# Tuning a streaming-encoder layer on eight cores: v's weights once per tile, and another tile for each first copy of the weights

## The reference, cut to what matters

```python
xn = rmsnorm(x, g_pre_mix)
z = xn @ w_in                       # (B,T,1024) @ (1024, 6*1024)
xa, ga, u, v, gates = jnp.split(z, [...], axis=-1)
xc, conv_new = causal_conv(xa, conv_prev, conv_w, conv_b)
hseq, h_last = rglru(xc, h0, w_a, b_a, w_x, b_x, lam)
o_a = (hseq * jax.nn.gelu(ga)) @ w_br_a                       # branch A
vn = layernorm(jax.nn.gelu(v), ln_g, ln_b)
o_b = (jax.nn.gelu(u) * spatial_gate(vn, w_s, b_s)) @ w_br_b  # branch B
g_a, g_b = jnp.split(jax.nn.sigmoid(gates), 2, axis=-1)
x = x + rmsnorm((g_a * o_a + g_b * o_b) @ w_out, g_post_mix)
gate, up = jnp.split(rmsnorm(x, g_pre_ffn) @ w_ffn_in, 2, axis=-1)
x = x + rmsnorm((jax.nn.silu(gate) * up) @ w_ffn_out, g_post_ffn)
```

## Time and profile before

| | |
|---|---|
| median of 3 runs | 2137.91 us (2136.51 to 2145.68) |
| the profiled execution | 2138.31 us |
| its span, slowest core (6) | 2136.8 us |
| spans of the eight cores | 2119.7 to 2136.8 us |
| TensorE busy | 2057.6 us (96%) |
| VectorE, ScalarE, Pool busy | 1127.0, 970.5, 548.4 us |
| the 16 DMA engines busy | 39.8% (casting queue) and 38.1% (SP's queue) |
| granted TensorE clock, mean | 0.990 |

### The profile page before, as it was taken

How to read it: one execution, slowest core, us unless ns; L and a number is a source line. 1 busy time by engine, 2 the same in 40 slices (tenths; PEclk the granted TensorE clock), 3 DMA queues, 4 the chain that set the end, 5 groups by cost and what they waited for, 6 DMA issues and landing times.

```text
span 2136.8 us, 35683 instructions; the slowest of 8 cores (2119.7 to 2136.8 us)
## 1 busy us (share of the span) xinstructions
PE 2057.6 (96%) x10775; PEld 962.6 (45%) x10775; DVE 1127.0 (53%) x1610; ACT 970.5 (45%) x1531; POOL 548.4 (26%) x920
## 2 busy tenths in 40 slices
PE   5998999998999999999999999999999999999998
PEld 2444445443444444444444444444444444444543
DVE  4863775236762377514774167722785248732542
ACT  3763873116741277313781157611784127711311
POOL 3323431223322243113431133211331022200200
PEclk9999999999999999999999999999999999999999
DMA  9998778889889998898988799858859466544353
GB/s 188 209 174 183 168 149 149 142 176 238 170 150 179 208 238 176 168 172 224 240 173 170 174 252 233 201 156 221 279 162 226 155 204 211 166 150 153 126 163 131
DMA packets 157768, 395.77 MB, mean 185 GB/s; under 512 B 18704, under 2 KB 18768, under 8 KB 157584
## 3 DMA queue, kind: packets, MB, share of 16 engines
q0 software_dynamic: 36368, 131.42, 39.8%
q1 hardware_dynamic: 121216, 262.08, 38.1%
HBM read 471.29 MB, written 53.54 MB: 246 GB/s over the span
## 4 chain that ended last, share of the span: by engine, by line
PE 87%; DMA 7%; issue 2%; DVE 1%; ACT 1%; POOL 1%; SPq 0%; DVEq 0%; ACTq 0%; POOLq 0%
PE ps L574 86%; DMA mring<-wsc 3%; DMA fring<-wt 3%; DMA xres<-xp 1%; PE ps L789 1%; DMA xpre<-xp 1%; DVE XC L888 0%; ACT junk L580 0%; DMA yp<-xres 0%; POOL stats L672 0%; ACT xsb L580 0%; POOL stats L675 0%; DVE hnT L792 0%; ACT xcb L580 0%; DVE xres L816 0%
## 5 line engine op out<-in xcount | busy, mean ns | idle before, releaser
L574 PE MATMUL ps<-hnT,fring 128*128 128x512 bf16 (+2 forms) x2880 | 631.5, 374 | 2.0 <-DVE hnT L792 1.6
L574 PE MATMUL ps<-xnT,mring 128*128 128x512 bf16 x2400 | 562.6, 380 | 3.6 <-DMA mring<-wsc 1.6
L574 PEld LDWEIGHTS ps<-hnT,fring 128*128 128x128 bf16 x2880 | 278.3, 98 | 330.2 <-issue 3.7
L580 ACT ACTIVATE T<-ps 128x512 f32<-128x512 f32 x247 | 146.1, 596 | 560.3 <-PE ps L574 534.5
L574 PEld LDWEIGHTS ps<-xnT,mring 128*128 128x128 bf16 x2400 | 229.5, 98 | 267.6 <-issue 11.9
L574 PE MATMUL ps<-fring,ffT 128*128 128x512 bf16 (+1 forms) x1424 | 325.5, 379 | 0.0
L1137 DVE SCALAR_TENSOR_TENSOR T<-T,ps 128x512 f32<-128x512 f32 x120 | 82.5, 688 | 381.6 <-PE ps L574 381.6
L632 POOL DMA_DIRECT2D fring<-wt x196 | 110.8, 565 | 509.5 <-PE ps L574 459.3
L1342 DVE SCALAR_TENSOR_TENSOR sgt<-sgt,ps 128x512 f32<-128x512 f32 (+2 forms) x182 | 122.2, 673 | 220.9 <-ACT sgt L580 204.4
L580 ACT ACT_TABLE_LOAD x164 | 210.4, 1283 | 26.4 <-PE ps L574 22.3
L574 PEld LDWEIGHTS ps<-fring,ffT 128*128 128x128 bf16 (+1 forms) x1424 | 139.3, 98 | 167.0 <-issue 0.4
(11 more groups left out here) (158 smaller groups left out, 2013.3 us busy)
## 6 DMA issues: line engine op xcount, KB each, us to landing
mring<-wsc SPq DMA_DIRECT2D x444, 256.0 KB, 5.9
fring<-wt POOLq DMA_DIRECT2D x196, 512.0 KB, 8.5
fring<-wsc SPq DMA_DIRECT2D x222, 256.0 KB, 3.2
mring<-wt POOLq DMA_DIRECT2D x53, 512.0 KB, 11.0
wsc<-fring SPq DMA_DIRECT2D x47, 512.0 KB, 8.8
xpre<-xp SPq DMA_DIRECT2D x30, 512.0 KB, 12.9
xres<-xp SPq DMA_DIRECT2D x29, 512.0 KB, 13.6
yp<-xres SPq DMA_DIRECT2D x29, 512.0 KB, 7.7
```

The lines of the kernel that those rows point to most:

```text
L574: P.op("pe", lambda e: e.matmul(out, lhsT=lhsT, rhs=rhs, start=start, stop=stop), reads=reads, writes=writes, cost=max(27.0, n / 2.4 + 2.5))
L580: P.op("act", lambda e: e.activation(out=out, in_=in_, func=func, **kw), reads=reads, writes=writes, cost=165.0 + 0.833 * n + 93.0 * aps + ...
```

## The change

In all tiles one `v_get(h)` now serves all subtiles: the former `s_v0` is the only `s_v`. The two float32 blocks that `T8` has no room for lie in `gsT` (blocks 0 to 3, seen as float32) instead of `sgt`. After the first tile, half 0 of v comes with XA 0 and half 1 with XA 4. `VM` is written by two operations of 512 columns a subtile instead of one of 1024. In `STORE_AT`, GTA and BRA are stored at use 0, in the first tile; XA, GA, V and BRB at use 1, in the second; GTB at 2; U and OUT at 3; the ffn pairs one or two uses earlier than before. The loads of `ln_g` and `ln_b` name all of `hnT` as written.

```diff
 def STORE_AT(q):
     pid = PAIRS[q][0]
     if pid >= W_FO:
-        return 3 if pid < W_FO + 8 else 4
+        return 1 if pid < W_FO + 8 else 2
     if pid >= W_FG:
         j = pid - W_FG
-        return 2 if j < 2 else 3 if j < 6 else 4 if j < 14 else 5
+        return 1 if j < 2 else 2 if j < 4 else 3 if j < 12 else 4
     if pid >= W_OUT:
-        return 4
-    if pid >= W_BRB or W_GTB <= pid < W_BRA:
         return 3
-    if pid >= W_BRA:
-        return 1
-    if pid >= W_GTA:
+    if W_GTA <= pid < W_GTB or W_BRA <= pid < W_BRB:
+        return 0
+    if W_GTB <= pid < W_BRA:
         return 2
-    return 0
+    if W_U <= pid < W_V:
+        return 3
+    return 1
...
+        gsF = gsT[:].rearrange("p c t -> p (c t)").bitcast(F32)
...
-                def s_v(p, h):
-                    got = v_get(h)
-                    for ss in range(2):
...
-                def s_v0(h, s):
+                def s_v(h, s):
                     if s == 0:
                         S["v", h] = v_get(h)
                     got = S["v", h]
...
-                    slot = (lambda n: (T8[:, n, :], ("T8", n)) if n < 4 else (sgt[:, n - 4, :], ("sgt", n - 4)))
+                    slot = (lambda n: (T8[:, n, :], [("T8", n)]) if n < 4 else
+                            (gsF[:, (n - 4) * 512:(n - 3) * 512], [("gsT", 2 * (n - 4)), ("gsT", 2 * (n - 4) + 1)]))
                     where = [slot(s), slot((4, 5, 0, 1)[s])]
...
-                    vu = [(0, 0), (0, 1), (1, 0), (1, 1)]
                     for c in range(NCH):
                         add(U, lambda c=c: s_xa(c))
-                        if c % 2 == 0:
-                            add(2 * U, lambda c=c: s_v(*vu[c // 2]))
+                        if c % 4 == 0:
+                            for s in range(NSUB):
+                                add(U, lambda c=c, s=s: s_v(c // 4, s))
```

More of the change, by code:

```diff
@@ L723, in row_loads @@
                 cdma(lambda e: e.dma_start(out=hist_s[:], in_=sc_in), writes=[("hist_s",)], after=P.mark())
-                cdma(lambda e: e.dma_start(out=lng_bc[0:64, :], in_=ln_g.partition_broadcast(64)), writes=K_hnT[0:2], nbytes=1 << 18, after=P.mark())
-                cdma(lambda e: e.dma_start(out=lnb_bc[0:64, :], in_=ln_b.partition_broadcast(64)), writes=K_hnT[2:4], nbytes=1 << 18, after=P.mark())
+                cdma(lambda e: e.dma_start(out=lng_bc[0:64, :], in_=ln_g.partition_broadcast(64)), writes=K_hnT, nbytes=1 << 18, after=P.mark())
+                cdma(lambda e: e.dma_start(out=lnb_bc[0:64, :], in_=ln_b.partition_broadcast(64)), writes=K_hnT, nbytes=1 << 18, after=P.mark())
                 dve(64, lambda e: e.memset(wsT[64:128, :, 0:64], 0.0), (), [("wsT",)])
@@ L958, in s_v0 @@
                     v_unit(got, lambda k: xnT[:, k, s * 128:(s + 1) * 128], 128, b, [("xnT", s)])
-                    v_evac(128, b, where[h][0], [where[h][1]], s, h)
+                    v_evac(128, b, where[h][0], where[h][1], s, h)
                     if h == 1:
-                        v_norm(128, s, [(where[x][0], [where[x][1]], VM[:, 2 * s + x, :], [("VM", 2 * s + x)]) for x in range(2)])
+                        v_norm(128, s, [(where[x][0], where[x][1], VM[:, 2 * s + x, :], [("VM", 2 * s + x)]) for x in range(2)])
                 def s_vs_out():
@@ L1243, in mixer @@
                         for s in range(NSUB + 1):
-                            add(U, lambda h=h, s=s: s_v0(h, s))
+                            add(U, lambda h=h, s=s: s_v(h, s))
                         if h == 0:
```

## The result

The changed kernel takes 0.9885 times the time of the kernel before, with a 95% interval of 0.984 to 0.993. Its profiled execution took 2117.59 us and another one 2115.32 us; the profiled execution before took 2138.31 us, so the two profiled ones differ by 20.7 us. The forecast was 2120 us, in a range of 2102 to 2145. Executions that were disturbed (a lower granted clock on one die) are left out of all comparisons, here three of the five of the change.

What follows compares the result with a forecast made beforehand. The prediction took TensorE, busy 96% of the span, as the bound, with only its stalls and the half clock behind them recoverable. Its terms -9 - 9 - 4 + 4 = -18 gave 2120 us, range 2102 to 2145.

Steps and rivals of the forecast that it cites:

- the forecast's own case: Whole kernel: -18 us to 2120 us, with its own range of 2110 to 2128; chance 0.45.
- First tile, -9: First tile: eight stores less remove two TensorE waits for casts and the half clock behind the second; -9 us.
- no wait for a cast before 60 us: Sign that the forecast is right: TensorE has no such wait in the first tile, and no clock of 0.57 there.
- v's loads, -9: Tile starts: v's fetches fall from 4 to 2 a tile, removing waits for v's weights and their clock loss; -9 us.
- the 4 that the prediction set: Sign that the forecast is right: TensorE's waits for `wsc` loads fall from 10.6 to under 4 us.
- Seams of tiles 3 and on, -4: Tiles 4 to 6: a lighter DMA queue may bring x's rows sooner, making tile 5's start like tile 6's; -4 us.
- The test of tile windows that lose under 2 us: Sign that the forecast is right: tile windows from tile 4 on lose under 2 us.
- Tile 1, +4: Tile 1: 12 pairs become casts with stores in its first 100 us, adding DMA work; +4 us, between -3 and +18.
- At nothing: `VM` by two operations, ScalarE's waits for `VM`, Pool's fewer casts and SP's added issues: all priced at no time.
- The rule on casts starved by VectorE: Tile 1: Pool-issued casts delayed by certain VectorE operations, an estimated 4 us more for 8 added casts; left out.
- The second rival: TensorE arrives earlier and waits for `xcb` and `xsb` instead; -4 us, 2134 us; chance 0.23.
- The third rival: Tile 1 runs short of weights, with Pool issuing for both rings in order; slower, 2166 us; chance 0.15.

Runs made afterwards that it cites:

- the table alone: The kernel before with the new `STORE_AT` only, v still fetched twice a tile; ratio 0.9979 to the kernel before (0.9967 to 0.9991), 4.5 us.
- v alone: The change with the old `STORE_AT`, so only v fetched once per tile; 2118.39 and 2118.13 us, beside a median of 2136.5 for the kernel before.
- the ring of 8: The change with 8 instead of 10 buffers in the mixer's ring, same bytes; ratio to the kernel before 0.9979, the change beside it 0.992.
- the second fetch back: The change with v's weights fetched again for subtiles 2 and 3 in all tiles after the first; ratio 1.0027 to the kernel before, profiled 2138.57 us.
- x's rows sooner: The change with tile 1's rows of x loaded earlier in the first tile; ratios 0.9904 and 0.9895 to the kernel before, beside 0.992 of the change.

## Why the prediction was right

The sum was -18 and the profiles differ by 20.7. The sign, the size and the forecast's own case came true. In part that is luck, since two misses cancel: tile 1, forecast at +4, came out at -2.5, and tiles 2 to 6, forecast at -13 (v's loads and the seams), at -8.9.

- **First tile, -9.** It gave 8.5 us here, 9.1 with the table alone, and 7.2 of it went when the stores came back. The stall at 52.2 us with its clock is gone, as the step said. The test "no wait for a cast before 60 us" failed by the wait of 3.42 us at 18.3 us. The rows of x of tile 1, 3.60 and 6.75 us with 18 us at a clock of 0.67, are what is late next. More than half of that loss was in the kernel before as well, and the step had not priced it.
- **v's loads, -9.** The term priced the starts of tiles 2 to 4. v alone gave 8.9 us in these tiles, as forecast, but 18 in all, with 3.1 more in the first tile, 1.9 in tile 1 and 4.2 in tile 5. In the whole change tiles 2 to 4 gave only 3.1: the table alone costs 2.6 there, and TensorE still waits 3.4 us in tile 4, for `xcb` and `xsb`. So the term is right for v alone, too large for the whole change in its own place, and too small for what v is worth: taking the single fetch out again cost 21 us by the profiled executions, 23 in tiles 1 to 4. The waits for `mring<-wsc` are 3.2 us, under the 4 that the prediction set, though with 2.1 on the other ring. That the fetch costs by what it keeps from being fetched ahead fits the ring of 8 and tile 3, but the bytes were not parted from it.
- **Seams of tiles 3 and on, -4.** Tiles 4, 5 and 6 gave -1.2, 5.2 and 0.6, together 4.6, and the place is the one named: tile 5's start became like tile 6's. But either part of the change does that by itself. The reason given, x's rows sooner on a lighter queue, was not shown. The test of tile windows that lose under 2 us holds for tiles 5 and 6, where TensorE waits 1.1 and 1.2 us, and not for tile 4.
- **Tile 1, +4.** The table alone lengthens it by 5.0 us, so this step's size was right for the table. What the step left out is v: in the whole change tile 1 is 2.5 shorter, and with the second fetch back it is 6.8 longer again. The share rose from 0.84 to 0.97, near the 1.0 forecast, and no wait for `mring<-wt` is in core 6's list.
- **At nothing.** VectorE's busy time rose by 3.8 us and ScalarE's fell by 1.4, with no cost to be seen; `VM` is in no wait of the list above.
- **The rule on casts starved by VectorE** (the Trainium skill, page "SBUF — State Buffer", section "SBUF: two separate sides"). By it tile 1 would have been longer by an estimated 4 us more, 8 in all for the table. The table alone cost 5.0 where the sum without the rule said 4, so it was not needed. No run tests it.
- **The second rival** wanted the waits to return under other names. That happened in part at the end of the first tile, and again with x's rows sooner; in the change itself `xcb` and `xsb` over ScalarE stayed at 24 us.
- **The third rival** needed over 15 us of waits in tile 1; the window of 203 to 326 us loses 1.0. It was not near: even with 8 casts more in tile 1 TensorE waited 1.6 us there.

Open: v alone and the table alone give 18 and 4.5 us, which is no more than the interval of the whole allows; by the stages they overlap in tile 5. How the second fetch's cost divides between DMA time, ring buffers and the planner's order was not settled in any tile. In tile 1 there is one thing more: the second fetch is no cast there, as was expected (the casts stay 205), but reads copies of v's weights that have only just been stored.

## What to carry to other kernels

A load that is made twice can be worth more than the waits that bear its name: here 18 us by itself, where all waits for loads into that ring were 10.6. Put it back by itself to price it, and look at the start of a tile, where the DMA engines are full and loads land late; in tiles with a share of 0.57 to 0.71 it was worth nothing. Where latencies stand in a row, removing one only shows the next.

Where a planner sets the order, each edit is two: what you changed, and the order that comes with it. Two looks guard against this. Look in the trace where the added work really ran before you read what it cost. And count the work on both sides of a boundary before you compare two stages.

## What the runs showed that was not expected

On the second chip the kernel before took 2177 to 2181 us (medians) instead of 2137. Windows of the change there, core 4, 1110 to 1150 us:

```profile
1110.00:1120.00 10.00, 10.00 (x48) 4.51 (x47) 4.21 (x7) 8.18 (x12) 2.28 (x6) 1.00 1.01 228
1120.00:1130.00 10.00, 10.00 (x42) 4.27 (x41) 8.36 (x11) 8.06 (x11) 4.41 (x5) 0.88 0.85 192
1130.00:1140.00 10.00, 10.00 (x46) 4.47 (x45) 5.97 (x10) 4.95 (x8) 0.88 (x3) 0.83 0.71 150
1140.00:1150.00 10.00, 10.00 (x57) 4.91 (x56) 7.57 (x11) 8.00 (x10) 4.46 (x5) 1.00 0.60 119
```

TensorE is busy all of each 10 us, and the granted clock reads 0.88 and 0.83 for a while: a lower clock with no idle time ahead of it, unlike the half clock behind the stalls. It is not a mix of the two levels of the first chip: the trace has a third value, 0.812. Core 4 had 28 such stretches, up to 15.1 us long; its mean clock was 0.959. On the first chip no core has one. The change is worth 0.992 of the time there and 0.9885 on the first chip, with intervals that overlap.

The second surprise is the price of order on SP's queue: 56 copies that were meant for seven tiles all ran in tile 1 and made its stage 68 us longer, with waits of TensorE under the name of VectorE's `mvt` (18.8 us).
